# The sum of squares of a head's outputs in a recurrent decoder: two single-pass products in place of one float32 product

## The reference, cut to what matters

```python
def head_rmsnorm(o, g):
    return o * lax.rsqrt(jnp.mean(o * o, axis=-1, keepdims=True) + EPS) * g.astype(jnp.float32)

o_hg = merge_heads(head_rmsnorm(o_hg, p['hgrn_out_norm'][l])) * jax.nn.silu(f32(hg))
```

## Time and profile before

| what | us |
|---|---|
| median of 3 runs | 3126.01 (3123.97 to 3126.93) |
| the profiled execution | 3129.89 |
| its span, first to last instruction | 3127.8 |
| PE busy in it | 3050.6 |
| POOL busy | 1899.0 |
| DVE busy | 1174.6 |
| ACT busy | 555.4 |

### The profile page before, as it was taken

One profiled execution on the slowest core, in us unless ns is written; L12 is line 12 of the kernel. 1 busy time (PEld: TensorE's weight loads), 2 busy tenths in 40 slices (PEclk: granted clock), 3 DMA queues, 4 the chain that ended last, 5 costly groups with the idle time before them and its releaser, 6 DMA issues.

```text
span 3127.8 us, 65933 instructions
## 1 busy us (share of the span) xinstructions
PE 3050.6 (98%) x24128; PEld 2950.4 (94%) x24128; DVE 1174.6 (38%) x1578; ACT 555.4 (18%) x867; POOL 1899.0 (61%) x1812
## 2 busy tenths in 40 slices
PE   7999999999999999999999999999999999999998
PEld 7999989989988999999899999999898889999997
DVE  4121275534324472121521214744353145621215
ACT  3000122131232311010110101321303322110001
POOL 5666675545443577676766667754545335776666
PEclk9999999999999999999999999999999899999999
DMA  3222232232222232222222222321312123322222
GB/s 122 88 87 88 88 123 75 73 101 69 83 68 72 90 119 84 93 85 91 88 88 88 87 88 88 123 73 63 115 66 83 55 77 104 103 88 88 88 89 94
DMA packets 115162, 276.37 MB, mean 88 GB/s; under 512 B 9240, under 2 KB 53152, under 8 KB 114720
## 3 DMA queue, kind: packets, MB, share of 16 engines
q1 hardware_dynamic: 65088, 237.01, 22.7%
q10 hardware_dynamic: 49888, 36.71, 3.8%
HBM read 255.16 MB, written 18.52 MB: 87 GB/s over the span
## 4 chain that ended last, share of the span: by engine, by line
PEld 45%; PE 41%; POOL 4%; DVE 4%; issue 3%; ACT 1%; PEldq 1%; POOLq 0%; ACTq 0%; DMA 0%; DVEq 0%
PEld dense L432 45%; PE dense L432 31%; POOL Wl L410 3%; POOL Wh L408 2%; PE SA L578 1%; PE SA L651 1%; PE SA L564 1%; PE SA L629 1%; PE SA L507 1%; DVE Hl L1032 1%; PE SB L647 1%; PE SA L632 1%; PE SA L549 0%; PE SA L496 0%; DVE tmp L1027 0%
## 5 line engine op out<-in xcount | busy, mean ns | idle before, releaser
L408 POOL TENSOR_SCALAR Wh<-raw 128x512 fp32r<-128x512 f32 x904 | 630.5, 697 | 1136.8 <-PEq L437 1019.7
L410 POOL TENSOR_TENSOR Wl<-raw,Wh 128x512 fp32r<-128x512 f32 x904 | 1268.3, 1403 | 75.5
L432 PE MATMUL dense<-Hh,Wh 128*128 128x272 f32 x3744 | 796.2, 294 | 20.7 <-DVE Hl L1018 11.1
L432 PE MATMUL dense<-Hh,Wl 128*128 128x272 f32 x3744 | 782.8, 291 | 0.0
L432 PE MATMUL dense<-Hl,Wh 128*128 128x272 f32 x3744 | 780.1, 290 | 0.0
L432 PEld LDWEIGHTS dense<-Hh,Wh 128*128 128x128 f32 x3744 | 596.8, 191 | 30.9 <-issue 12.8
L432 PEld LDWEIGHTS dense<-Hl,Wh 128*128 128x128 f32 x3744 | 596.6, 191 | 0.0
L432 PEld LDWEIGHTS dense<-Hh,Wl 128*128 128x128 f32 x3744 | 592.8, 191 | 0.0
L432 PE MATMUL dense<-Mh,Wh 128*128 128x272 f32 x1536 | 316.1, 288 | 4.0 <-DVE X L1462 2.0
L432 PE MATMUL dense<-Ml,Wh 128*128 128x272 f32 x1536 | 316.4, 287 | 0.0
L432 PE MATMUL dense<-Mh,Wl 128*128 128x272 f32 x1536 | 315.2, 287 | 0.0
(11 more groups left out here) (337 smaller groups left out, 2784.8 us busy)
## 6 DMA issues: line engine op xcount, KB each, us to landing
raw<-wst SPq DMA_DIRECT2D x452, 512.0 KB, 3.2
x_keep<-X ACTq DMA_DIRECT2D x2, 2176.0 KB, 7.9
X<-x_keep ACTq DMA_DIRECT2D x16, 272.0 KB, 3.3
sst<-st_h ACTq DMA_DIRECT2D x8, 512.0 KB, 4.3
s_h<-sst ACTq DMA_DIRECT2D x8, 512.0 KB, 3.5
sst<-st_c ACTq DMA_DIRECT2D x8, 512.0 KB, 4.0
s_c<-sst ACTq DMA_DIRECT2D x8, 512.0 KB, 3.2
X<-xT ACTq DMA_DIRECT2D x4, 544.0 KB, 7.7
```

The costliest lines, as they stand in the source:

```text
L408: pool.tensor_scalar(Wh[:, j, cs], raw[:, j, cs], 1.0, 0.0, ALU.mult, ALU.add).then_inc(glink, 1)
L410: pool.tensor_tensor(Wl[:, j, cs], raw[:, j, cs], f32(Wh[:, j, cs]), ALU.subtract).then_inc(glink, 1)
L432: mm = pe.matmul(dps[slot][:, a, 0:HALF], w[:, ring, w0:w0 + 128], x[:, k, a * HALF:(a + 1) * HALF], start=(k == 0 and n == 0), stop=(k == ...
```

## The change

The squares are split by DVE in step `o` into a rounded part (`sqh`) and the rest (`sql`), both float32r, and PE multiplies each with a float32r matrix of ones into the same sum. Two tiles lie over parts of `tmp` that are free then; `sql` is written over the squares. In the first two branches ACT squares ahead of its copies, and DVE waits for the squares in step `o`, as it did in the third. `num_sq` now counts 24 instructions in a layer in place of 8.

```diff
+        onesr, _ = sb("onesr", [P, P], F32R, tmp_at + 4 * TOK * 4 + (DEC_B * (SMP + DEC_T) + P) * 4)
+        sqh, _ = sb("sqh", [P, TOK], F32R, tmp_at + 5 * TOK * 4)
+        sql, _ = sb("sql", [P, TOK], F32R, tmp_at + 2 * TOK * 4)
...
                     for a in range(2):
-                        mm = pe.matmul(SA[:, a, 0:HALF], ones[:, :], tmp[:, 2, a * HALF:(a + 1) * HALF],
-                                       start=True, stop=True)
+                        ts = slice(a * HALF, (a + 1) * HALF)
+                        pe.matmul(SA[:, a, 0:HALF], onesr[:, :], sqh[:, ts], start=True, stop=False)
+                        mm = pe.matmul(SA[:, a, 0:HALF], onesr[:, :], sql[:, ts], start=False, stop=True)
...
+                    if br < 2:
+                        act.activation(tmp[:, 2, 0:SEQ], SA[:, 0, :], ACT.Square).then_inc(num_sq, 1)
+                        act.activation(tmp[:, 2, SEQ:TOK], SA[:, 1, 0:SMP], ACT.Square).then_inc(num_sq, 1)
                     ch.did(act.activation(O[:, h, 0:SEQ], SA[:, 0, :], ACT.Copy))
                     ch.did(act.activation(O[:, h, SEQ:TOK], SA[:, 1, 0:SMP], ACT.Copy))
-                    if br < 2:
-                        ch.did(act.activation(tmp[:, 2, 0:SEQ], SA[:, 0, :], ACT.Square))
-                        ch.did(act.activation(tmp[:, 2, SEQ:TOK], SA[:, 1, 0:SMP], ACT.Square))
...
+                    if br == 0 and h == 0:
+                        ch.did(dve.tensor_copy(onesr[:, :], ones[:, :]))
...
                     ch.did(TT(vblk[:, :].rearrange("p (b v) -> p b v", v=P),
...
+                    if br < 2:
+                        dve.wait_ge(num_sq, L * 24 + (br * HEADS + h) * 2 + 2)
+                    ch.link(dve.tensor_copy(sqh[:, :], tmp[:, 2, :]))
+                    ch.did(TT(sql[:, :], tmp[:, 2, :], f32(sqh[:, :]), ALU.subtract))
                     if h < HEADS - 1:
                         own_queries(br, h + 1)
```

More of the change, by code:

```diff
@@ L1338, in step @@
                         ch.link(TT(nb, nb, tmp[:, 5, :], ALU.max))
-                        dve.wait_ge(num_sq, (L * HEADS + h) * 2 + 2)
+                        dve.wait_ge(num_sq, L * 24 + (br * HEADS + h) * 2 + 2)
                         ch.link(STT(tmp[:, 2, :], nb, HUGE, tmp[:, 2, :], ALU.min, ALU.add))
```

## The result

| | median us | runs | lowest to highest |
|---|---|---|---|
| before | 3127.86 | 8 | 3122.49 to 3135.34 |
| after | 3137.16 | 8 | 3131.14 to 3140.44 |

The ratio is 1.0027, with a 95% interval of 1.0015 to 1.0040: the change makes the kernel slower by 8.4 us (4.7 to 12.5); the medians differ by 9.3. The forecast was 3128.6 in a range of 3120.5 to 3134, so the time lies above the range. The profiled execution of after took 3137.55 us, its span 3135.7. Its lines are three further down up to line 652, so 432 is now 435 and 647 is 650.

A forecast was written before the change was run, and what follows sets the result against it. PE, busy for 98% of the span, was taken to bound the kernel. The terms -10.1 + 8.8 + 1.4 + 2.5 = +2.6 us on 3126.0 gave 3128.6 us, range 3120.5 to 3134.

The forecast's parts named there:

- PE time removed: Line 651, the sum of squares: four float32r matmuls per head at 0.125 us, not 0.23; 10.1 us less over 24 heads.
- The rival that they keep the old spacing: Line 651: the new products stay 0.23 us apart, nothing is gained, 3138.7 us; chance 0.03.
- Work added on DVE: Step `o`: each head gets a copy (0.43 us) and a subtraction; with hand-over 1.2 us on a free port.
- The waits: PE ahead of `z`: copy and subtraction not hidden in some heads of each branch; 4.4 us a layer, 8.8 in all.
- the small-wait rival: Ahead of `z`: DVE gets its turn before POOL's second instruction, 2.5 us a layer, no clock falls, 3121 us; chance 0.20.
- What `m` takes back: Third branch, heads 0 and 1: DVE's `z` comes late and `m` waits for it; 1.4 us in all.
- The rival that DVE bounds the whole third branch: All eight heads of that branch pay for copy and subtraction: 7 to 13 us more, 3136 to 3141; chance 0.11.
- The clock: Behind longer waits ahead of `z`, head 0 of branches 0 and 2: clock falls to 0.5; 2.5 us taken.
- The upper end that the prediction worked out for this term: Clock falls behind PE's waits ahead of `z`: six stretches at half clock, 8 us.
- The chance of slower through the clock: The part of the forecast's 0.66 chance in which clock falls make the kernel slower: 0.06.

The follow-up runs named there:

- the filled kernel: The changed kernel with matmuls whose result nobody reads put on PE ahead of its wait for DVE in three late heads; 0.9997 of before.
- the pair without the new products: The changed kernel with DVE's copy and subtraction kept, but the squares multiplied in one float32 product as before; 1.0049 of before.

## Why the prediction was wrong

**PE time removed: right.** 10.1 us were forecast; a head without a new wait has 0.41 us less, and with the clock held the products bring 9.7 us, give or take 5.7. The rival that they keep the old spacing falls.

**Work added on DVE: right.** With POOL idle the copy takes 0.44 us (0.43 taken) and the subtraction 0.73.

**The waits: right, head by head.** `z` comes later than before by 0.81 us in branch 0 head 0 (0.8 forecast), 1.14 in head 3 (1.1), 0.27 in branch 1 head 0 (0.25) and 2.03 in branch 2 head 0 (2.1); branch 2 head 2 has none of its 0.1. Over both layers that is 8.5 us against 8.8. DVE and POOL take turns as the prediction says, so the small-wait rival falls. The Trainium skill's rule, SBUF — State Buffer, "Who interferes with whom", agrees, and of its two readings the first holds: the copy is held up too, at 0.85 us, so its exception for a copy outside the two-port modes doesn't apply here.

**What `m` takes back: too big, and another wait in its place.** 1.4 us were forecast. With the clock held `m` waits 6.1 us against 5.7, so 0.4 us; the state query waits 0.9 to 1.1 us for the load of the state, which the prediction left out. The two errors nearly cancel, and that is luck. The rival that DVE bounds the whole third branch falls (heads 1 and 2 each gain 0.4 us), but in head 0 the rows speak for it once the wait ahead of `z` is taken away (27.8 us, `m` waiting for DVE).

**The clock: this is the step that failed.** Without it the forecast's sum is +0.1 us, and the filled kernel, whose heads have no such fall, measures 0.9997. The prediction saw the falls, and where; its term of 2.5 us was mis-sized. It priced a fall at one stretch of 3.4 us with 1.3 us lost, half of that absorbed by `m`. The trace shows 6.8 to 10.2 us at half clock for one wait, in one of them all of `z` and 20 dense matmuls; the cost, after everything absorbed, is 2.2 to 3.4 us for each of three falls, 8.5 us by the spacing of the heads and 9.4 (3.8 to 15) by the ratios. How often branch 0 head 0 brings a fall, one in three, fits the traces: two in six. The upper end that the prediction worked out for this term, 8 us, was about the true value; the range took only 3 us of it on top. The chance of slower through the clock, 0.06, was too low by the same step. Of the 8.6 us between the forecast and the median measured, this term makes about 6, and 1.9 lie in the three runs that the forecast stood on.

## What to carry to other kernels

Work moved from a saturated PE to an idle engine is paid by the head with the least slack, so price it head by head, and where two engines share a port, instruction by instruction. A new wait on PE counts twice: its own length, and the half clock behind it; for a wait of about 3 us, 2 of them new, the second part was 1.5 to 3.4 us here, and it was got back by giving PE something to do in the wait. Before splitting a number in two to keep its rest, ask whether the rest is needed: the single rounded product gained 14 us where the split lost 8.

## What the runs showed that was not expected

- A fall of the clock can outlast the wait by far, and by different amounts: at waits of 3.0 us it was 10.2, 6.8 and twice 3.4 us at 0.5 (after, and the pair without the new products). Waits of 1.3 us were followed by a fall twice in six.
- A wait removed ahead of one step came back ahead of later ones: moving the sum back took 8 us of idle time from `z` and put 7 in `o`, 3 at the query and 4 at `m`.
- Taking 3 us of idle time out of the kernel before shows in the spacing of its heads (3.1 us) and not in its median (1.0000, 0.9989 to 1.0012): the spacing is the finer measure.
- POOL is held up as well: when it asks while DVE is busy, its first instruction takes 1.47 us in place of 0.62, and ends behind DVE's next one.
